# Sample projections by column groups, key/value weights in 16 KB runs, and buffer records split by later writes in an encoder step on eight cores

## The chip, the cores and the metric

The kernel runs on the 8 cores of one Trainium2 chip, in two dies of four. Each core works on its own data: no core waits for another. The metric is the device time of the slowest core, in microseconds (us). The shortened names in the profile are PE for TensorE (matmuls), PEld for its weight loads, DVE for VectorE, ACT for ScalarE, POOL for GpSimd and SP for SyncE.

## The reference

One step of an encoder layer is computed for two groups that share all weights: 4 prompt streams of 4096 frames, and 16 running streams of 16 frames each (the "sample" group, with pooling and convolution states and a cached memory). Cut to what matters here:

```python
def cross_attn(xn, mem_k, mem_v, w_q, w_co):
    q = jnp.einsum('btd,dhe->bthe', xn, w_q)
    s = jnp.einsum('bthe,bmhe->bhtm', q, mem_k).astype(jnp.float32) * (XHEAD_DIM ** -0.5)
    p = jax.nn.softmax(s, axis=-1).astype(mem_v.dtype)
    o = jnp.einsum('bhtm,bmhe->bthe', p, mem_v)
    return jnp.einsum('bthe,hed->btd', o, w_co)

def encoder_layer(x, ...):
    # 1: pooling and short gated convolution
    proj = rmsnorm(x, g_mix_pre) @ w_in                  # 1024 -> 2048
    ...
    x = x + rmsnorm(merged @ w_out, g_mix_post)
    # 2: cross-attention into 256 memory tokens, 4 heads of 256
    x = x + rmsnorm(cross_attn(rmsnorm(x, g_x_pre), mem_k, mem_v, w_q, w_co), g_x_post)
    # 3: squared-ReLU MLP, 1024 -> 4096 -> 1024
    hid = jnp.square(jax.nn.relu(rmsnorm(x, g_ff_pre) @ w_up))
    x = x + rmsnorm(hid @ w_down, g_ff_post)
# prompt group: mem_k = rmsnorm(mem) @ w_k and mem_v = rmsnorm(mem) @ w_v are computed and returned
```

Each core takes half a prompt stream (2048 frames) and two of the sample streams (32 rows).

## The kernel before, in words

**Tiling.** The 2048 prompt rows of a core are 4 tiles of 512 (`NT`, `TN`). Activations are held transposed in `xT` (feature chunks of 128 on the partitions), so a projection of 128 output features is 8 matmuls of a 128x128 weight block against 512 moving columns. The 32 sample rows ride along in the same way, transposed in `xTe`.

**Stages.** First comes the mixer for the four tiles, with the key/value projections of the memory (`kv_block(0..3)`, two halves of w_k, then two of w_v) put between the pooling groups of tile 2. Then w_q and the keys are folded into `Am` (`fold_a`) and the values and w_co into `Bm` (`fold_b`), and attention runs over the tiles in the order 2, 3, 0, 1. In the second of its four rounds `smp_q` and `smp_attn` do the sample rows. Last comes the MLP over tiles 0 to 3: 32 up chunks (`up_chunk`, 8 matmuls each, then ReLU on ACT and the square on DVE), then the down projection (`out_tile`, 32 chunks deep).

**Sample rows.** `smp_q` makes the queries as 8 output blocks of 128 features, each of 8 matmuls with a 128x128 block of w_q as weights and 32 moving columns. `up_smp(k, ps)` does the same for the four 128-feature chunks of w_up piece k, called after the four prompt chunks of piece k of tile 0, for all 8 pieces. The down projection and the two other output projections of the sample rows (`out_smp`) work the other way round: the 32 sample columns are the weights, 256 columns of the weight matrix move, and four such matmuls go to four groups of 32 array columns (PSUM partitions 0-31, 32-63, ...). Results there lie with 32 rows on 4 groups of partitions.

**Weights on the way.** w_up comes in 8 pieces of 1 MB (as bf16) into three slots `up0..2`. Piece k+3 goes into the slot of piece k and is issued once all its readers are done (`load_up`). The first four pieces of w_down are loaded before the MLP. The last four, `wdn4..7`, lie where attention had its buffers and are issued when piece 7 of w_up has landed (`load_down(4, 8, op)`). For tile 0 `out_tile` is called with `late`: it does the first half of the depth for two row blocks before it touches the second half. All these loads convert float32 to bf16 and are issued by POOL, in order. w_k and w_v come in two halves each into `wkv0` and `wkv1`, in runs of 512 floats (2 KB); the w_v halves are issued when the w_k half in the same buffer has been used.

**Order.** The engines' programs are written out by a planner. `Prog.add` records each operation with its reads and writes. `Tracker` holds a record for each write (its rectangle, its writer and those who read it since), and from overlaps the operation gets its dependences. A record is dropped when one later write covers it whole. `Prog.schedule` then lists the operations in order of time: on each engine, of those ready by its own cost figures, the one that comes first in the program. Its figure for DMAs is 280 GB/s for runs of 2 KB and 345 GB/s for runs of 16 KB (bytes of the float32 source), plus 2.6 us, and where several queues are active they share in proportion to their run length (2 KB counts 0.5, SP's 4 KB counts 1, 16 KB counts 4). The engines then run these lists in order, waiting only on semaphores.

**Lines.** Matmuls are recorded at L670, transposes at L675, ACT operations at L699, copies at L733 (ACT), L735 (DVE) and L737 (POOL), DVE operations at L706, L715, L720 and L725, and all DMAs at L744.

Of the kernel before, what the change touches and what calls it, by code (L numbers as in the profile page):

```python
# [7 lines left out]
F32 = mybir.dt.float32  # L8
BF16 = mybir.dt.bfloat16
F32R = mybir.dt.float32r  # L10
AF = mybir.ActivationFunctionType
ALU = mybir.AluOpType
# [3 lines left out]
D = 1024  # L16
# [6 lines left out]
NS = 32  # L23
# [172 lines left out]
class Prog:  # L196
# [9 lines left out]
    def add(self, opts, reads=(), writes=(), nbytes=0, lead=0, after=None, desc=4096):  # L206

        op = Op()
        op.idx = len(self.ops)
        op.opts = opts  # L210
        op.is_dma = nbytes > 0
        op.bytes = nbytes
        op.desc = desc
        op.deps = {} if after is None else {after: "raw"}
        op.prio = op.idx - lead
        op.ps_new = []
        op.ps_acc = set()
        op.eng = None
        self.ops.append(op)
        multi = len(opts) > 1  # L220
        eng = None if (op.is_dma or multi) else opts[0][0]

        def dep(p, kind):
            if p is not None and p is not op and op.deps.get(p) != "raw":
                op.deps[p] = kind
        for ap in list(reads) + list(writes):
            if isinstance(ap, PV):
                op.ps_acc.add(ap.ps)
                if ap.ps.id not in self.ps_seen:
                    self.ps_seen.add(ap.ps.id)  # L230
                    op.ps_new.append(ap.ps)
        for ap in reads:
            sp, rects = rects_of(ap)
            for r in rects:
                for rec in list(self.tr.find(sp, r)):
                    dep(rec.writer, "raw")
                    if sp[0] == "P":
                        for rd, k in rec.readers.items():
                            if k != eng or eng is None:
                                dep(rd, "war")  # L240
                    rec.readers[op] = eng
        for ap in writes:
            sp, rects = rects_of(ap)
            for r in rects:
                for rec in list(self.tr.find(sp, r)):
                    dep(rec.writer, "war")
                    for rd in rec.readers:
                        dep(rd, "war")
                    q = rec.rect
                    if r[0] <= q[0] and r[1] >= q[1] and r[2] <= q[2] and r[3] >= q[3]:  # L250
                        rec.dead = True
                self.tr.put(sp, r, op)
        return op

# [280 lines left out]
def build_program():  # L535
# [4 lines left out]
    def din(name, shape):  # L540
        return nc.dram_tensor(name, list(shape), F32, kind="ExternalInput")
# [10 lines left out]
    gd = {n: din(n, [1, D]) for n in gnames}  # L552
    win_d = din("w_in", [7, 128, 4096])
    wout_d = din("w_out", [128, 8192]); wco_d = din("w_co", [128, 8192])
    wk_d = din("w_k", [16, 128, 512]); wv_d = din("w_v", [16, 128, 512])
    wq_d = din("w_q", [16, 128, 512]); wqT_d = din("w_qT", [16, 128, 512])
    wup_d = din("w_up", [8, 128, 4096]); wdn_d = din("w_down", [8, 128, 4096])
    wpool_d = din("w_pool", [128, 512])
# [39 lines left out]
    rts = fix("rts", 16 * NS, BF16)  # L598
# [41 lines left out]
    wkv = [at("wkv%d" % i, W0 + i * 8192, 4096, BF16) for i in range(2)]  # L640
# [5 lines left out]
    wq = at("wq", A0 + 82 * K, 8 * D, BF16)  # L646
# [21 lines left out]
    def mm(out, lhsT, rhs, start, stop, share=1):  # L668
        n = ncols(rhs) / share
        P.add([("pe", lambda e, L: e.matmul(L(out), lhsT=lhsT, rhs=rhs, start=start, stop=stop,  # L670
                                            skip_group_check=True), max(0.03, n * 0.000421 + 0.001))],
              reads=[lhsT, rhs], writes=[out])

    def tr(out, in_, idn):
        P.add([("pe", lambda e, L: e.transpose(out=L(out), in_=in_, identity=idn),  # L675
                0.065 if in_.dtype == BF16 else 0.25)], reads=[in_, idn], writes=[out])
# [7 lines left out]
    def act(out, in_, func, scale=1.0, bias=None, accum=None, lead=0):  # L684
        rdl = [in_]
        wr = [out]
        kw = {}
        if bias is not None:
            kw["bias"] = bias
            rdl.append(bias)  # L690
        if not isinstance(scale, float):
            rdl.append(scale)
        if accum is not None:
            kw["accum_out"] = accum
            wr.append(accum)
        n = ncols(in_)

        def f(e, L):
            return e.activation(out=L(out), in_=L(in_), func=func, scale=scale, **kw)  # L699
        P.add([("act", f, c_act(n) + (0.19 if accum is not None else 0.0) + (0.06 if bias is not None else 0.0))], reads=rdl, writes=wr, lead=lead)  # L700

    def tt(out, in0, in1, op, eng="dve", per=1.0):
        n = ncols(out)
        opts = []
        if "dve" in eng:
            opts.append(("dve", lambda e, L: e.tensor_tensor(out=L(out), in0=L(in0), in1=L(in1), op=op), c_dve(n, per)))  # L706
        if "pool" in eng:
            opts.append(("pool", lambda e, L: e.tensor_tensor(out=L(out), in0=L(in0), in1=L(in1), op=op),  # L708
                         0.18 + n * 0.00168))
        P.add(opts, reads=[in0, in1], writes=[out])  # L710
# [18 lines left out]
    def copy(out, in_, eng="dve", per=1.0, after=None):  # L729
        n = ncols(out)  # L730
        opts = []
        if "act" in eng:
            opts.append(("act", lambda e, L: e.activation(out=L(out), in_=L(in_), func=AF.Copy, scale=1.0), c_act(n)))  # L733
        if "dve" in eng:
            opts.append(("dve", lambda e, L: e.tensor_copy(out=L(out), in_=L(in_)), c_dve(n, per)))  # L735
        if "pool" in eng:
            opts.append(("pool", lambda e, L: e.tensor_copy(out=L(out), in_=L(in_)), 0.18 + n * 0.002))  # L737
        return P.add(opts, reads=[in_], writes=[out], after=after)
# [10 lines left out]
    def load(out, in_, nbytes, q="sp", lead=LEAD, rd=False, after=None, desc=4096):  # L749
        return dma(q, out, in_, nbytes, rd=rd, lead=lead, after=after, desc=desc)  # L750

    def wload(dst, src, b0, b1, after=None):
        return load(dst.rearrange("p (b c) -> p b c", c=512), src[b0:b1].rearrange("b p c -> p b c"),
                    (b1 - b0) * 262144, q="pool", after=after, desc=2048)

    def r3(ap, n):
        return ap.rearrange("p (c t) -> p c t", c=n)
# [438 lines left out]


    def kv_loads(k, after=None):
        wload(wkv[k % 2][:, :], wk_d if k < 2 else wv_d, 8 * (k % 2), 8 * (k % 2) + 8, after)

    def kv_mem():
        for i in range(2):
# [55 lines left out]
    def attn_head(t, hh):  # L1258
# [16 lines left out]
            tt(p2, p2, r.unsqueeze(1).to_broadcast([128, 2, TN]), ALU.mult)  # L1275
        return finish

    def smp_loads():
        wload(kTs[:, :], ckT, 0, 8)
        wload(vSs[:, :], cv, 0, 8)  # L1280

    def smp_q():
        ps = PS(1)
        for j in range(8):
            for kc in range(8):
                mm(ps.v(0, 128, j * NS, (j + 1) * NS), wqk(j, kc), xTek(0, NS)(kc), kc == 0, kc == 7)
        copy(qTs[:, :], ps.v(0, 128, 0, 8 * NS), eng="act dve")

    def smp_attn():

# [31 lines left out]
    up_slot = {}  # L1322
# [14 lines left out]
        act(r, ps.v(0, 128, 0, TN), AF.Relu)  # L1337
        tt(hid(c), r, r, ALU.mult, per=0.5)

    def up_smp(k, ps):  # L1340
        s = up_slot[(0, k)]
        for jj in range(4):
            c = k * 4 + jj
            cl = c % 16
            for kc in range(8):
                mm(ps.v(0, 128, cl * NS, (cl + 1) * NS), s[:, jj * 1024 + kc * 128: jj * 1024 + (kc + 1) * 128],
                   xTek(0, NS)(kc), kc == 0, kc == 7)
        if k % 4 == 3:
            act(rts[:, :], ps.v(0, 128, 0, 512), AF.Relu)
            tt(hids[:, (k // 4) * 512:(k // 4 + 1) * 512], rts[:, :], rts[:, :], ALU.mult, per=0.5)  # L1350

    wd = lambda kc, h: dparts[kc // 4][:, (kc % 4) * D + h * 512: (kc % 4) * D + (h + 1) * 512]

# [123 lines left out]
            load_down(0, 4, xl[3])  # L1477
    load_gp("g_ff_post")
    load_gps(2)
    ups = None  # L1480
    for t in range(NT):
        for k in range(8):
            for jj in range(4):
                up_chunk(t, k * 4 + jj)
            if t == 0:
                if k % 4 == 0:
                    ups = PS(1)
                up_smp(k, ups)
            n = k + 3
            if n < 8:  # L1490
                op = load_up(t, n)
                if t == 0 and n == 7:
                    load_down(4, 8, op)
            elif t + 1 < NT:
                load_up(t + 1, n - 8)
        if t + 1 < NT:
            pre_tile(t + 1, 2, xT[(t + 1) % 2])
        out_tile(t, hid, 32, wd, gslot["g_ff_post"], yp, late=t == 0)
        if t == 0:
            out_smp(lambda kc: hids[:, kc * NS:(kc + 1) * NS], 32, wd)  # L1500
            dma("sp", ysm[:, :], Xs[:, :], NS * 4096, wr=False)
        if t + 2 < NT:
            load_tile(t + 2, x2)
# [117 lines left out]
```

How the kernel before makes its waits and increments, by code:

```python
        def run(e, eng):  # L474
            seen = {}
            ends = sorted(dma_last.items(), key=lambda kv: kv[1].end)
            for n, op in enumerate(seqs[e]):
                if e == "sp" and n == len(seqs[e]) - 1:
                    for k, last in ends:
                        if last.end < op.start - SETTLED and seen.get(k, 0) < last.semval:
                            eng.wait_ge(dsem[k], last.semval)
                            seen[k] = last.semval
                waits = {}
                for p in plan[op]:
                    k, v = (p.sem, p.semval) if p.is_dma else (p.eng, p.sigval)
                    if seen.get(k, 0) >= v:
                        continue
                    if waits.get(k, 0) < v:
                        waits[k] = v
                for k, v in waits.items():
                    eng.wait_ge(dsem[k] if isinstance(k, tuple) else esem[k], v)
                    seen[k] = v
                ins = op.fn(eng, lambda x: x.resolve(psum) if isinstance(x, PV) else x)
                if op.is_dma:
                    ins.then_inc(dsem[op.sem], 16)
                elif op.needs_signal:
                    ins.then_inc(esem[e], 1)
            if e == "sp":
                for k, last in ends:
                    if seen.get(k, 0) < last.semval:
                        eng.wait_ge(dsem[k], last.semval)
```

## Time and profile before

| | |
|---|---|
| device time, median of 3 runs | 848.71 us (848.17 to 849.42) |
| profiled execution, device time | 848.66 us |
| its span (slowest core, core 6) | 847.1 us |
| spans of the eight cores | 841.2 to 847.1 us |
| PE busy | 813.7 us (96%) |
| DVE, ACT, POOL busy | 391.1, 390.8, 102.2 us |
| HBM read, written by the core | 144.38 MB, 18.07 MB |

The profiled execution lies 0.05 us under the median of the runs, so its rows can be set against it directly. Its device time is 1.5 us more than its span. A busy figure for PE is the union of matmuls in flight; a single matmul of 512 columns is shown as 379 ns long, while one starts every 0.216 us.

### The profile page before, as it was taken

Reading aid. Unit: us, or ns where it says so; the run is one execution under the profiler, and the core shown is the slowest. Engines: PE = TensorE matmul, PEld = TensorE weight load, DVE = VectorE, ACT = ScalarE, POOL = GpSimd, SP = SyncE. Lnnn points to the kernel's source line nnn. Section 1 sums busy time; section 2 is a strip of 40 time slices with the busy share of each in tenths; the row PEclk is TensorE's granted clock in tenths of the full one; section 3 lists DMA queues with packets and bytes.
Section 4 is the critical chain, followed back from the end, with each engine's and each line's share of the span. In section 5 each row is a group of like instructions: output and inputs, shape, how many; then the busy total and the mean of one; then the engine's idle time right before and its main releaser. Section 6 shows DMA issues by size and latency. Waiting matters only on the chain.

```text
span 847.1 us, 13900 instructions; the slowest of 8 cores (841.2 to 847.1 us)
## 1 busy us (share of the span) xinstructions
PE 813.7 (96%) x4708; PEld 391.2 (46%) x4708; DVE 391.1 (46%) x540; ACT 390.8 (46%) x806; POOL 102.2 (12%) x179
## 2 busy tenths in 40 slices
PE   3889999899999999999999999999999999999997
PEld 1444454444644454455454454444444444444443
DVE  4886885568966666765222222241222321222112
ACT  3586786758867556675332233332233411233101
POOL 7612103002111113110010000000000000000000
PEclk9999999999999999999999999999999999999999
DMA  9999439550396606993889716881248820185011
GB/s 196 199 229 202 129 117 208 111 81 1 65 149 113 199 26 187 161 174 84 149 144 165 186 72 132 154 147 53 99 96 156 156 68 26 50 150 100 1 50 50
DMA packets 29793, 102.39 MB, mean 121 GB/s; under 512 B 2386, under 2 KB 13266, under 8 KB 24348
## 3 DMA queue, kind: packets, MB, share of 16 engines
q0 software_dynamic: 19408, 67.32, 46.4%
q1 hardware_dynamic: 9740, 32.75, 11.5%
q10 hardware_dynamic: 576, 1.44, 0.5%
q8 instruction: 39, 0.64, 0.3%
q14 instruction: 30, 0.25, 0.1%
HBM read 144.38 MB, written 18.07 MB: 192 GB/s over the span
## 4 chain that ended last, share of the span: by engine, by line
PE 83%; DMA 11%; DVE 2%; issue 2%; POOL 1%; ACT 1%; another core or an unknown queue 0%; DVEq 0%; ACTq 0%; POOLq 0%
PE ps L670 80%; DMA X<-xp 4%; DMA wdn<-w_down 4%; PE ps L675 2%; DMA wkv<-w_v 2%; DMA up<-w_up 1%; POOL win L744 0%; DVE X L725 0%; ACT junk L699 0%; POOL wdn L744 0%; DVE O L706 0%; DVE z L725 0%; DVE z L706 0%; DVE V L706 0%
## 5 line engine op out<-in xcount | busy, mean ns | idle before, releaser
L670 PE MATMUL ps<-wdn,hid 128*128 128x512 bf16 x1024 | 222.3, 379 | 0.7 <-DMA wdn<-w_down 0.7
L670 PE MATMUL ps<-xT,up 128*128 128x512 bf16 x1024 | 222.6, 379 | 0.0
L670 PEld LDWEIGHTS ps<-wdn,hid 128*128 128x128 bf16 x1024 | 99.9, 98 | 120.4 <-issue 1.2
L670 PEld LDWEIGHTS ps<-xT,up 128*128 128x128 bf16 x1024 | 99.7, 98 | 119.1 <-issue 0.2
L706 DVE TENSOR_TENSOR O<-ps,gp 128x1024 f32<-128x1024 f32 (+1 forms) x49 | 58.3, 1200 | 191.0 <-PE ps L670 122.0
L699 ACT ACTIVATE rt<-ps 128x512 bf16<-128x512 f32 x128 | 76.4, 597 | 142.2 <-PE ps L670 138.3
L670 PE MATMUL ps<-xT,win 128*128 128x512 bf16 x512 | 122.1, 384 | 13.5 <-DMA win<-w_in 12.6
L706 DVE TENSOR_TENSOR hid<-rt 128x512 bf16<-128x512 bf16 x128 | 54.4, 425 | 157.8 <-ACT rt L699 156.0
L699 ACT ACTIVATE sqj<-ps 128x1024 bf16<-128x1024 f32 (+1 forms) x33 | 32.8, 994 | 173.2 <-PE ps L670 171.0
L670 PEld LDWEIGHTS ps<-xT,win 128*128 128x128 bf16 x512 | 49.4, 98 | 71.6 <-issue 17.7
L725 DVE SCALAR_TENSOR_TENSOR X<-O,st,X 128x1024 f32<-128x1024 f32 (+1 forms) x49 | 62.8, 1294 | 4.6 <-DVE O L706 3.8
L744 POOL DMA_DIRECT2D up<-w_up x32 | 17.2, 539 | 378.5 <-PE ps L670 364.9
L706 DVE TENSOR_TENSOR xT<-ps,cst 128x1024 bf16<-128x1024 bf16 x44 | 53.1, 1219 | 20.4 <-PE ps L675 20.2
L670 PE MATMUL ps<-wout,mg 128*128 128x512 bf16 x256 | 58.1, 379 | 3.3 <-DMA wout<-w_out 2.6
L699 ACT ACTIVATE xs<-X 128x1024 bf16<-128x1024 f32 x40 | 41.9, 1050 | 35.4 <-DMA X<-x 31.7
L670 PE MATMUL ps<-xT,Am 128*128 128x512 bf16 x256 | 58.3, 379 | 0.0
L670 PE MATMUL ps<-Bm,mg 128*128 128x512 bf16 x256 | 58.2, 379 | 0.0
L670 PEld LDWEIGHTS ps<-wout,mg 128*128 128x128 bf16 x256 | 24.6, 98 | 31.7 <-issue 3.9
L670 PEld LDWEIGHTS ps<-xT,Am 128*128 128x128 bf16 x256 | 24.2, 98 | 28.5 <-issue 1.7
L670 PEld LDWEIGHTS ps<-Bm,mg 128*128 128x128 bf16 x256 | 24.1, 98 | 27.2 <-issue 0.8
L708 POOL TENSOR_TENSOR psm<-mg 128x512 fp32r<-128x512 bf16 x16 | 19.3, 1208 | 108.8 <-ACT st L699 69.5
L675 PEld LDWEIGHTS ps<-idb,xs 128*128 128x128 bf16 (+1 forms) x412 | 26.2, 98 | 10.2 <-issue 2.0
(184 smaller groups left out, 687.1 us busy)
## 6 DMA issues: line engine op xcount, KB each, us to landing
up<-w_up POOLq DMA_DIRECT2D x32, 1024.0 KB, 9.9
x<-X SPq DMA_DIRECT2D x16, 512.0 KB, 4.2
X<-x SPq DMA_DIRECT2D x16, 512.0 KB, 4.5
wdn<-w_down POOLq DMA_DIRECT2D x8, 1024.0 KB, 30.0
yp<-X SPq DMA_DIRECT2D x15, 512.0 KB, 2.7
X<-xp POOLq DMA_DIRECT2D x8, 512.0 KB, 44.5
X<-xp SPq DMA_DIRECT2D x8, 512.0 KB, 4.4
win<-w_in POOLq DMA_DIRECT2D x4, 768.0 KB, 26.9
```

Of the source, the lines that this page charges most:

```text
L670: P.add([("pe", lambda e, L: e.matmul(L(out), lhsT=lhsT, rhs=rhs, start=start, stop=stop, skip_group_check=True), max(0.03, n * 0.000421 + ...
L675: P.add([("pe", lambda e, L: e.transpose(out=L(out), in_=in_, identity=idn), 0.065 if in_.dtype == BF16 else 0.25)], reads=[in_, idn], wri ...
L699: return e.activation(out=L(out), in_=L(in_), func=func, scale=scale, **kw)
L706: opts.append(("dve", lambda e, L: e.tensor_tensor(out=L(out), in0=L(in0), in1=L(in1), op=op), c_dve(n, per)))
L708: opts.append(("pool", lambda e, L: e.tensor_tensor(out=L(out), in0=L(in0), in1=L(in1), op=op), 0.18 + n * 0.00168))
L725: return P.add([("dve", lambda e, L: e.scalar_tensor_tensor(out=L(out), in0=L(in0), scalar=scalar, in1=L(in1), op0=op0, op1=op1), c_dve(nc ...
L744: return P.add([(q, lambda e, L: e.dma_start(out=out, in_=in_), 0.5 + nbytes / desc * 0.0005 if q == "pool" else 0.43)], reads=[in_] if rd ...
```

## The change

Four edits:

1. `smp_q` takes the queries in column groups: 8 depth steps of 4 matmuls (32 sample columns as weights, 256 moving columns of w_q, one group of 32 array columns for each head). The 128x256 result is copied to `rts[:, 0:256]`, turned by two 128x128 transposes (new function `turn_blocks`) and copied to `qTs`.
2. `up_smp(k)` does the same for pieces k and k+1 of w_up together, and is called after the prompt chunks of piece k for even k. So it reads slot k+1 as well, before the prompt chunks of piece k+1. ReLU and square are done on the 128x256 result, two transposes and a copy put it into `hids`.
3. w_k and w_v are stored as [2, 128, 4096], and each half is loaded in runs of 16 KB (4096 floats a partition) by `load` instead of `wload`.
4. In `Prog.add`, a write in SBUF that covers all rows of a record and some of its columns drops the record, and puts records for the columns left of it and right of it, with the old writer and the old readers.

```diff
-                    if r[0] <= q[0] and r[1] >= q[1] and r[2] <= q[2] and r[3] >= q[3]:
+                    if r[0] <= q[0] and r[1] >= q[1] and (sp[0] == "S" or r[2] <= q[2] and r[3] >= q[3]):
                         rec.dead = True
+                        for lo, hi in ((q[2], r[2]), (r[3], q[3])):
+                            if lo < hi:
+                                self.tr.put(sp, (q[0], q[1], lo, hi), rec.writer).readers.update(rec.readers)
...
-    wk_d = din("w_k", [16, 128, 512]); wv_d = din("w_v", [16, 128, 512])
+    wk_d = din("w_k", [2, 128, 4096]); wv_d = din("w_v", [2, 128, 4096])
...
     def kv_loads(k, after=None):
-        wload(wkv[k % 2][:, :], wk_d if k < 2 else wv_d, 8 * (k % 2), 8 * (k % 2) + 8, after)
+        load(wkv[k % 2][:, :], (wk_d if k < 2 else wv_d)[k % 2], 2097152, q="pool", after=after, desc=16384)
...
+    def turn_blocks(rows, dst):
+        ps = PS(1)
+        for q in range(2):
+            tr(ps.v(0, 128, q * 128, (q + 1) * 128, BF16), rows[:, q * 128:(q + 1) * 128], idb[:, :])
+        copy(dst.rearrange("p (g q t) -> p g q t", g=4, q=2),
+             ps.v(0, 128, 0, 256, BF16, lambda a: a.rearrange("p (q g t) -> p g q t", q=2, g=4)), eng="act dve")
...
     def smp_q():
         ps = PS(1)
-        for j in range(8):
-            for kc in range(8):
-                mm(ps.v(0, 128, j * NS, (j + 1) * NS), wqk(j, kc), xTek(0, NS)(kc), kc == 0, kc == 7)
-        copy(qTs[:, :], ps.v(0, 128, 0, 8 * NS), eng="act dve")
+        for kc in range(8):
+            for hh in range(4):
+                w = r3(wq[:, :], 8)[:, 2 * hh:2 * hh + 2, kc * 128:(kc + 1) * 128]
+                mm(ps.v(32 * hh, 32 * hh + 32, 0, 256, F32, lambda a: r3(a, 2)), xTek(0, NS)(kc), w, kc == 0, kc == 7, share=3)
+        q = rts[:, 0:256]
+        copy(q, ps.v(0, 128, 0, 256), eng="act dve")
+        turn_blocks(q, qTs[:, :])
...
-    def up_smp(k, ps):
-        s = up_slot[(0, k)]
-        for jj in range(4):
-            ...
+    def up_smp(k):
+        ps = PS(1)
+        for kc in range(8):
+            for g in range(4):
+                w = r3(up_slot[(0, k + g // 2)][:, :], 4)[:, 2 * (g % 2):2 * (g % 2) + 2, kc * 128:(kc + 1) * 128]
+                mm(ps.v(32 * g, 32 * g + 32, 0, 256, F32, lambda a: r3(a, 2)), xTek(0, NS)(kc), w, kc == 0, kc == 7, share=3)
+        r, h = rts[:, 0:256], rts[:, 256:512]
+        act(r, ps.v(0, 128, 0, 256), AF.Relu)
+        tt(h, r, r, ALU.mult, per=0.5)
+        turn_blocks(h, hids[:, k * 128:(k + 2) * 128])
...
-            if t == 0:
-                if k % 4 == 0:
-                    ups = PS(1)
-                up_smp(k, ups)
+            if t == 0 and k % 2 == 0:
+                up_smp(k)
```

## Rows read from the trace of the kernel before

**Rows 1.** The page: busy time, and PE's granted clock in 40 slices.
```profile
PE 813.7 (96%) x4708; PEld 391.2 (46%) x4708; DVE 391.1 (46%) x540; ACT 390.8 (46%) x806; POOL 102.2 (12%) x179
...
PEclk9999999999999999999999999999999999999999
```
**Rows 2.** Span and mean granted clock of the cores: two of the eight.
```profile
core 3: 845.2 us, clock 0.997
...
core 6: 847.1 us, clock 1.000
```
**Rows 3.** Who PE waited for, core 6: total us, times, longest us.
```profile
PE ps L670 <- DMA win<-w_in: 12.9, 2, 12.6
PE ps L670 <- DMA wout<-w_out: 2.6, 1, 2.6
PE ps L670 <- DMA wkv<-w_v: 2.2, 2, 2.0
...
PE ps L670 <- DMA wdn<-w_down: 0.7, 1, 0.7
```
**Rows 4.** Groups of instructions by form: busy us, mean ns | idle before.
```profile
L670 PE MATMUL ps<-xTe,up 128*128 128x32 bf16 x256 | 7.7, 176 | 0.0
```
**Rows 5.** Timeline of PE: start us, us until the last end, count; sample products.
```profile
412.65 0.96 PE L670 MATMUL ps<-xTe,up 128*128 128x32 bf16 x32
413.46 7.07 PE L670 MATMUL ps<-xT,up 128*128 128x512 bf16 x32
...
312.71 5.77 PE L670 MATMUL ps<-Bm,mg 128*128 128x512 bf16 x26
318.41 1.06 PE L670 MATMUL ps<-wco,mgs 128*32 128x256 bf16 x32
319.40 0.82 PE L670 MATMUL ps<-xT,Am 128*128 128x512 bf16 x3
...
502.35 3.68 PE L670 MATMUL ps<-wdn,hids 128*32 128x256 bf16 x128
505.96 1.68 PE L670 MATMUL ps<-xT,up 128*128 128x512 bf16 x7
```
**Rows 6.** Timeline of all engines at the start of the MLP.
```profile
382.98 1.97 PE L670 MATMUL ps<-xTe,up 128*128 128x32 bf16 x72
383.04 1.21 DVE L706 TENSOR_TENSOR xT<-ps,cst 128x1024 bf16<-128x1024 bf16 x1
...
384.80 0.38 PE L670 MATMUL ps<-xT,up 128*128 128x512 bf16 x1
```
**Rows 7.** The chain that ended last: the two DMAs in tile 0's MLP.
```profile
422.29 9.16 DMA up<-w_up
...
434.14 31.72 DMA wdn<-w_down
```
**Rows 8.** Timeline of PE around these two DMAs.
```profile
421.18 7.07 PE L670 MATMUL ps<-xT,up 128*128 128x512 bf16 x32
...
450.64 14.62 PE L670 MATMUL ps<-wdn,hid 128*128 128x512 bf16 x67
466.00 19.37 PE L670 MATMUL ps<-wdn,hid 128*128 128x512 bf16 x89 [0.73 <-DMA wdn<-w_down]
```
**Rows 9.** Timeline of POOL: issues of w_up pieces 3 and 4.
```profile
394.01 0.58 POOL L744 DMA_DIRECT2D up<-w_up  x1 [25.04 <-PE ps L670]
399.44 0.53 POOL L744 DMA_DIRECT2D up<-w_up  x1 [4.86 <-PE ps L670]
```
**Rows 10.** Timeline of POOL and PE: the w_v loads and their first readers.
```profile
129.25 0.95 POOL L744 DMA_DIRECT2D wkv<-w_v  x1 [22.91 <-PE ps L670]
...
137.76 0.91 POOL L744 DMA_DIRECT2D wkv<-w_v  x1 [0.55 <-PE ps L675]
...
148.56 3.61 PE L670 MATMUL ps<-wkv,mT 128*128 128x512 bf16 x16 [0.18 <-DMA wkv<-w_v]
...
158.50 3.61 PE L670 MATMUL ps<-wkv,mT 128*128 128x512 bf16 x16 [2.00 <-DMA wkv<-w_v]
```

More of the change, by code:

```diff
@@ L1338, in up_chunk @@
         tt(hid(c), r, r, ALU.mult, per=0.5)
-    def up_smp(k, ps):
-        s = up_slot[(0, k)]
-        for jj in range(4):
[L1343 to L1350, printed above, removed]
+    def up_smp(k):
[8 more added lines that the diff above has]
+        turn_blocks(h, hids[:, k * 128:(k + 2) * 128])
     wd = lambda kc, h: dparts[kc // 4][:, (kc % 4) * D + h * 512: (kc % 4) * D + (h + 1) * 512]
@@ L1479, in build_program @@
     load_gps(2)
-    ups = None
     for t in range(NT):
@@ L1548, in oct, with sides @@
         return f(a.reshape(128, 8, 4096).transpose(1, 0, 2))
+    def sides(w):
+        return f(chunks(f(w).reshape(D, D), 512).reshape(128, 2, 4096).transpose(1, 0, 2))
     def blk(a):
@@ L1558 @@
         "w_out": f(rows(w_out[0])).reshape(128, -1),
-        "w_k": blk(chunks(f(w_k[0]).reshape(D, D), 512)), "w_v": blk(chunks(f(w_v[0]).reshape(D, D), 512)),
+        "w_k": sides(w_k[0]), "w_v": sides(w_v[0]),
         "w_q": blk(chunks(f(w_q[0]).reshape(D, D), 128)),
```

## The prediction

> **What bounds the kernel now.** I read the page first: PE is busy for 813.7 of 847.1 us and at full clock (2.4 GHz) in every slice, while ACT and DVE are under half [rows 1]. So PE's list is the spine, and the question for each edit is whether PE's next wait moves with it. Then the cores: the slowest is core 6, 1.9 us behind core 3 [rows 2]. Then who PE waited for on core 6 [rows 3]: 12.9 us for the first w_in pieces, which no edit touches, 2.6 us for w_out, 2.2 us for w_v and 0.7 us for w_down. These last three, 5.5 us together, are what sets core 6 behind the best cores. Last the chain of waits, which shows that within the MLP of tile 0 two DMAs and not PE carry the time: w_up piece 7 for 9.16 us and then the last four w_down pieces until 465.9 us [rows 7]. After that PE runs without a wait to the end.
>
> The sums below are made against the profiled execution: device time 848.66, of which 847.1 is core 6's span and 1.5 lies around it. The runs' median is 848.71, so nothing is converted.
>
> **Edit 1, the sample queries.** The old form: 32 matmuls of 32 columns take from 412.65 to 413.46, 0.81 us or 25.3 ns each [rows 5]. `smp_q` has 64: 1.62 us. The new form stands in the trace as the w_co product of the sample rows, 32 matmuls of 256 columns in four column groups: from 318.41 to 319.40. A full matmul of 512 columns starts every 0.2158 us ((14.62 - 0.379)/66 of the 67 in rows 8; one is shown 0.379 us long). The 26 ahead of the group start at 312.71 and are through at 318.32, so the group costs 1.08 us [rows 5]. I add two transposes of 128 columns, a quarter of a full matmul each (54 ns), 0.11 us. New 1.19 us, saved 0.43 us. The copy, the second copy and the wait between them lie on ACT and DVE; the attention products behind them have 28 and more ready matmuls of the prompt in front of them. If that cover were gone it would cost about 1.5 us once. Attention is PE-bound here, so I count 0.43 us in full.
>
> The longer group of the same form, 128 matmuls, takes 3.61 us [rows 5]. Two equations (0.99 = 32x + c, 3.61 = 128x + c) give x = 27.3 ns and c = 0.12 us, and 0.09 us are lost on entering. So a group pays some 0.2 us for going in and out. The Trainium skill (TensorEngine Tiling, "Key Properties") says that changing the tiling mode drains TensorE; the trace agrees, with these 0.2 us. Without the drain five new groups would be 1.0 us cheaper; I use the row, which contains it.
>
> **Edit 2, the sample up products.** 256 matmuls [rows 4] at 25.3 ns are 6.5 us. The new form is four groups at 1.19 us, 4.8 us. PE has 1.7 us less to do. Whether that is time depends on where.
>
> (a) Ahead of the MLP. 72 of the small matmuls stand between 382.98 and 384.80 while `xT` for tile 0 is being finished: DVE's last piece ends at 383.04 + 1.21 = 384.25 and the first prompt chunk starts at 384.80 [rows 6]. With one group of at most 1.08 us for pieces 0 and 1 PE is done by about 384.1 and then waits for `xT`, until about 384.38. The MLP starts 0.42 us earlier, and the rest of what is saved there is idle time.
>
> (b) From there to the release of the slot of piece 4, which lets w_up piece 7 be issued. Before: 384.80 to 421.18, 36.4 us [rows 6, 8]: 160 prompt matmuls (34.5 us) and the 73 small ones of pieces 2 to 4 (1.85). After: 34.5 us, the groups for pieces 2 and 3 and for 4 and 5 (2.16) and four transposes (0.22), 36.9 us. That is 0.5 us more, since pieces 0 to 2 were done ahead of the MLP before and piece 5 is now done ahead of the release. So the release moves by +0.5 - 0.42 = +0.1 us.
>
> (c) From the release PE's need and the DMA run a race. DMA: piece 7 lands at 431.45, the four w_down pieces are issued then, and the last has landed at 465.9, 44.8 us after the release, during which the loads are back to back (31.7 us for four, some 8 us each) [rows 7]. PE: 44.1 us, from 421.18 until it stands at 465.27 with 88 down matmuls done and waits 0.73 us [rows 8]. In the new kernel three sets of small ones go (3 x 0.81 = 2.43), one group and four transposes come (1.08 + 0.22): 43.0 us, 1.1 us less. The DMA part is the same. So the wait for w_down grows from 0.7 to about 1.9 us, and everything saved behind the release is lost to it. Behind 466 the work is the same as before.
>
> So edit 2 gives -0.1 us net (a loss of 0.1 on its own, bounds -0.5 to +1.7 saved, the latter if the DMAs shrink with PE). The new reads of slot k+1 cost nothing by the rows: piece 5's slot is free at about 384.4 + 20.7 + 1.1 = 406.2, the load is issued 0.8 us later and lands 9.2 us after that (as piece 7 did [rows 7]), at 416.2; its first reader, the group behind piece 4, starts at about 420.1. Cover gone, it would cost the difference.
>
> **Edit 3, key/value weights.** POOL's issue of such a load is 0.95 us in runs of 2 KB and 0.53 to 0.58 in runs of 16 KB [rows 9, 10]; POOL is 12% busy, so that is nothing. The w_k halves are last in POOL's queue at 20 us and first used at 124: nothing. The w_v halves are issued at 129.25 and 137.76 and land just before 148.56 and 158.50, 19.3 and 20.7 us later, beside stores and loads of X on SP's queue [rows 10]. A lone 16 KB load of this size takes 9.16 us [rows 7]. If only the landing moved, 2.2 us of waits would go. But PE's list moves too. PE came to the two blocks 19.1 and 18.7 us after the issues (148.38 and 156.50, taking off the waits), which is where the planner, with its 280 GB/s and a share of a third against SP, expected them. With 345 GB/s and a share of four fifths it expects them about 10.5 us after the issue, so it puts the blocks at about 139.8 and 148. The first load lands between 9.2 us (alone) and 19.3 us (as now) after its issue; by the nearest row, the 9.16 us one, stretched by X's traffic, I take 11 us, 140.3. The second cannot start until the first is through: about 8 us later plus some of X's traffic, 148 to 152, I take 149.8. PE then waits some 2 us in all (bounds 0 and 10), against 2.2 us now: 0.2 us gained. Cores without such a wait before (core 3 is one) get about 1 us of it, and stay under core 6.
>
> **Edit 4, the tracking.** It removes dependences only. An example: an old record of the first stage reaches from `rt0` into the slot `up0`, so loads into `up0` also wait for the readers of `rt`. Piece 3 is issued at 394.01, 2.3 us after its chunk's matmuls ended (384.80 + 32 x 0.2157 = 391.7), piece 4, in `up1`, only 0.8 us after its own (398.6) [rows 9]. The load comes up to 1.5 us earlier, but PE waits for no w_up piece [rows 3], and piece 7 lies in `up1`. The same in attention and between the two `rt` buffers: ACT and DVE have slack. I take 0, with 1 us to either side, because the planner's lists are made anew and small shifts follow.
>
> **Sum.** -0.43 (edit 1) + 0.1 (edit 2) - 0.2 (edit 3) + 0 = -0.55 us: **848.1 us**. What a measurement of this kernel can tell from no change is 0.2%, 1.7 us, so this is "within".
>
> **Rivals.** (A) *Everything saved counts.* The DMA chain of the MLP gives way with PE, and w_v is in time: -0.43 - 1.7 - 2.2 = -4.3 us on core 6. Core 3 has no w_v wait and saves only 2.1, and becomes the slowest at 843.1 + 1.5: 844.6 us. For it: core 6 is slowest by DMA waits alone [rows 2, 3]. Against it: between 434 and 466 the DMAs run back to back [rows 7], and PE's list follows the planner.
> (B) *The w_v blocks are put too early, the slower side.* Place: kv_block(2) and (3). X's stores and loads on SP take as much of the DMAs as now, and w_v lands at about 144 and 153 while PE comes at 139.8 and 148: 5 us of waits for 2.2 now, on every core. 848.1 + 3.0 = 851.1 us. It decides from 4.5 us of waits in all, where the time leaves 0.2%. For it: the planner's figure for 16 KB loads is short, 6.1 us of transfer where the w_down pieces took about 8 [rows 7]; for 2 KB loads the sharing made up for it. The Trainium skill (DMA: Bandwidth & Descriptors, "Queues, rings and completion order") says that each DMA engine takes its queues in turn by packets. By that rule SP would not be pushed back to a fifth, and this rival would gain; no row here shows the turns.
> (C) *The change does not do what it says for PE*: a group of four column tiles, with moving operands in two pieces of 128 columns, runs at half the pace of the rows, 60 ns a matmul. Then each group costs 0.9 us more; of the five those of the queries, of the first pieces (0.6 of it) and the two in (b) count, 3.3 us: 851.4 us. Against it: the rows for both out-products, which differ only in having one piece.
> (D) *The new lists* happen to shift POOL's psum additions or the w_down issues by one or two us, to either side: 846 or 850 us.
>
> **Numbers.** Forecast 0.47. A (all or most of it) 0.25, B 0.16, C 0.02, D 0.10, of which 0.05 on the fast side, 0.04 on the slow side and 0.01 inside the 0.2%. Faster is 0.25 + 0.05 = 0.30, slower 0.16 + 0.02 + 0.04 = 0.22, within 0.48. The range reaches into A and B: 844.7 to 851.0. The forecast's own is 846.8 to 849.6.
>
> **What would show it.** Sample groups of 32 matmuls in about 1.0 to 1.1 us with four of them in the MLP and one in attention. PE's first prompt chunk of the MLP right after DVE's last `xT` piece. PE's wait for w_down at about 1.9 us on core 6, and present on cores that had none or little. PE reaching the w_v blocks about 10 us after the issues, and waits for them on most cores. The forecast is wrong if w_down's wait does not grow, if the w_v waits are gone or above 4 us, or if PE shows a wait of over 1 us in a place not named here.

## The result, and the profile after

The changed kernel takes 854.13 us (median of 7 runs; 852.13 and up) where the kernel before takes 848.60 (7 runs, 848.17 to 849.45): the ratio is 1.0057 [1.0046, 1.0068], 4.8 us slower. One run of the seven (879.67 us) had one die at a lower clock from end to end and is left out of the ratio, and on the first two chips of the experiments below one die was like that in every run, so that their table compares die 0 as well, over the runs in which that die is undisturbed, and e5 to e8 have no ratio. The forecast was 848.1 with a range up to 851.0. It was wrong, on the slow side.

The profiled run took 854.79 us. Its page (busy time and instructions; share of the chain of waits), against [rows 1]:

```profile
PE 811.1 (95%) x4472; PEld 389.2 (46%) x4558; DVE 393.7 (46%) x544; ACT 391.2 (46%) x811; POOL 99.4 (12%) x179
...
PE 85%; DMA 9%; DVE 2%; issue 2%; ACT 1%; POOL 1%; another core or an unknown queue 0%; ACTq 0%; DVEq 0%; POOLq 0%
```

PE has 2.6 us less to do and the kernel takes about 5 us more, so the loss is idle time or clock. The cores, as in [rows 2]:

```profile
core 3: 852.8 us, clock 0.993
core 4: 853.2 us, clock 0.990
...
core 7: 846.7 us, clock 0.994
```

Six of the eight cores (spans from 846.0 to 853.2) are later than the 847.1 of the slowest before. The mean granted clock is 0.990 to 0.998, where it was 0.996 to 1.000. Who PE waited for on core 4, as in [rows 3]:

```profile
PE ps L673 <- DMA win<-w_in: 15.5, 2, 14.8
PE ps L673 <- DMA wkv<-w_v: 3.4, 1, 3.4
PE ps L673 <- ACT st L702: 2.1, 1, 2.1
PE ps L673 <- DMA wdn<-w_down: 1.6, 1, 1.6
```

Two rows are the news. The wait for w_v was on three cores before (2.0, 2.2 and 1.0 us) and is on all eight now (5.2, 3.4, 5.4, 3.4, 3.4, 5.2, 2.1, 2.0). And `ACT st` was no row of before at all; it is on six cores now, with 1.0 to 2.1 us.

**Where it arises.** I took four points on every core, and the means over the cores: the first matmul of the `wkv` blocks is 1.5 us later than before, the first `Am` product (about 245 us before) 5.8 us later, the first prompt chunk of the MLP 5.4, the end 5.9. So nearly all is lost ahead of 251 us, and most of it in the stage with the key and value blocks. The w_v loads and their first reader there, POOL and then PE of core 4 (compare [rows 10]):

```profile
133.59 0.60 POOL L747 DMA_DIRECT2D wkv<-w_v  x1 [24.47 <-PE ps L673]
...
142.31 0.57 POOL L747 DMA_DIRECT2D wkv<-w_v  x1
```
```profile
143.94 0.38 PE L673 MATMUL ps<-pld,wpool 128*128 128x512 bf16 x1
147.71 4.66 PE L673 MATMUL ps<-wkv,mT 128*128 128x512 bf16 x14 [3.40 <-DMA wkv<-w_v]
```

Taking off the wait, PE came at 144.3, 10.7 us after the issue. The chain has the load itself:

```profile
133.59 13.98 DMA wkv<-w_v
```

And the 14 matmuls behind the wait take until 152.21, 4.5 us where 3.0 is their pace at full clock. The busy time of the engines in steps of 2 us shows why; the column after POOL is the granted clock (PE, PEld, DVE, ACT, POOL busy, clock, DMA share, GB/s):

```profile
144.00:146.00 2.00, 0.31 (x2) 0.00 (x0) 0.58 (x1) 2.00 (x4) 0.00 (x0) 1.00 0.95 207
146.00:148.00 2.00, 0.29 (x1) 0.14 (x2) 1.90 (x3) 0.37 (x1) 0.50 (x1) 0.83 1.08 291
148.00:150.00 2.00, 2.00 (x6) 0.73 (x5) 0.16 (x1) 0.00 (x0) 0.21 (x1) 0.50 0.97 166
150.00:152.00 2.00, 2.00 (x10) 0.78 (x8) 0.00 (x0) 0.68 (x2) 0.00 (x0) 0.82 1.14 174
152.00:154.00 2.00, 2.00 (x12) 0.94 (x11) 0.76 (x2) 1.74 (x3) 0.00 (x0) 1.00 0.97 209
```

The clock goes to 0.50 (1.2 GHz) as PE comes out of the wait and is back at 1.00 (2.4 GHz) by 152: six matmuls in two microseconds, where the last row has twelve. The Trainium skill (TensorE: Matmul & The Clock Gate, "Part 1") describes a clock gate with just these two levels, which goes to the lower one when PE has stood idle; the trace agrees, since the steps at 0.83 and 0.82 are the ones in which it switched.

The wait of 2.1 us for `ACT st` stands earlier. ACT and PE of core 4:

```profile
88.11 1.06 ACT L702 ACTIVATE xs<-O 128x1024 bf16<-128x1024 f32 x1 [2.98 <-DMA O<-mem]
```
```profile
91.40 0.38 PE L673 MATMUL ps<-sq,ones 128*128 128x512 bf16 x1 [2.15 <-ACT st L702]
```

ACT's list now has the square of the memory rows ahead of their landing. ACT stands 2.98 us, the work of the gates is queued behind it, and PE waits for that. The experiments with the planner's new figure (e1, e5, e7, e9, e10, below) have this wait on some of their cores too; the kernel before and the experiments with the old figure have it on none.

**The account, means over the cores.** Between 120 and 170 us PE is idle 3.85 us where it was 0.86: +3.0. The clock of that stretch was 1.00 on every core and is 0.97 on six cores and 0.93 on two; of 50 us that is 1.7 and 3.4, mean 2.1, a little of which lies inside the waits. Ahead of it +1.5. Between 170 and 240 the idle time falls from 1.9 to 0.35: −1.5. And the new list has six matmuls of 512 columns more (`ps<-wco,vT`) and ten transposes fewer between the first `wkv` matmul and the first `Am` product: +0.75, a shift and not a loss. Together +5.9 for the 5.8 found.

### The profile page after: what moved, and what is told of

It is laid out like the page before. It is cut to its first block, busy times and chain, and to the rows that moved or that the text cites. A ratio compares the mean times of both kernels' runs of the same rounds, so it can differ in the third digit from the quotient of the medians.

```text
span 853.2 us, 13491 instructions; the slowest of 8 cores (846.0 to 853.2 us)
## 1 busy us (share of the span) xinstructions
PE 811.1 (95%) x4472; PEld 389.2 (46%) x4558; DVE 393.7 (46%) x544; ACT 391.2 (46%) x811; POOL 99.4 (12%) x179
## 4 chain that ended last, share of the span: by engine, by line
PE 85%; DMA 9%; DVE 2%; issue 2%; ACT 1%; POOL 1%; another core or an unknown queue 0%; ACTq 0%; DVEq 0%; POOLq 0%
PE ps L673 82%; DMA wdn<-w_down 4%; DMA win<-w_in 3%; PE ps L678 2%; DMA wkv<-w_v 2%; DMA up<-w_up 1%; DVE mg L709 0%; DVE sAB L1048 0%; DVE O L709 0%; DVE X L728 0%; DVE pld L728 0%; ACT sq L702 0%; POOL win L747 0%; ACT rf L702 0%
## 5 line engine op out<-in xcount | busy, mean ns | idle before, releaser
L673 PEld LDWEIGHTS ps<-wdn,hid 128*128 128x128 bf16 x1024 | 99.9, 98 | 121.2 <-issue 2.1
L673 PE MATMUL ps<-xT,win 128*128 128x512 bf16 x498 | 122.6, 390 | 16.3 <-DMA win<-w_in 14.8
L678 PEld LDWEIGHTS ps<-idb,xs 128*128 128x128 bf16 (+1 forms) x412 | 26.3, 98 | 10.5 <-issue 1.6
L678 PE MATMUL ps<-idb,xs 128*128 128x128 bf16 (+1 forms) x412 | 30.6, 218 | 0.0
```

## The experiments

Twelve runs, in three sets of four on one chip each (e1 to e4, e5 to e8, e9 to e12), beside the kernel before. The last column compares the slowest core of die 0: the difference of the means to the kernel before beside it, with its 95% interval.

| | what | device us, before beside it | ratio | die 0, slowest core, us |
|---|---|---|---|---|
| e1 | edit 3 alone | 856.39, 855.06 | 1.0017 [0.9999, 1.0036] | +3.83 [3.08, 4.72] |
| e2 | edit 4 alone | 854.33, 855.06 | 0.9994 [0.9978, 1.0009] | −0.32 [−1.11, 0.47] |
| e3 | edits 1 and 2 | 855.58, 855.06 | 1.0005 [0.9988, 1.0022] | −1.57 [−2.04, −1.04] |
| e4 | edit 3, old figure to the planner | 854.93, 855.06 | 1.0008 [0.9994, 1.0022] | −1.22 [−1.72, −0.70] |
| e5 | old loads, new figure | 872.93, 866.31 | | +10.40 [9.27, 11.53] |
| e6 | all but edit 3 | 863.24, 866.31 | | −0.35 [−1.55, 0.72] |
| e7 | all but edit 4 | 866.93, 866.31 | | +2.48 [1.55, 3.44] |
| e8 | all, old figure | 861.41, 866.31 | | −1.61 [−2.49, −0.77] |
| e9 | all, again | 852.15, 848.52 | 1.0044 [1.0032, 1.0056] | +3.96 [3.08, 4.91] |
| e10 | all, PE kept busy in the wait | 852.39, 848.52 | 1.0044 [1.0028, 1.0059] | +4.01 [2.8, 5.1] |
| e11 | edits 1 to 3, old figure | 845.97, 848.52 | 0.9969 [0.9956, 0.9981] | −2.37 [−2.89, −1.85] |
| e12 | edit 1 alone | 848.92, 848.52 | 1.0004 [0.9992, 1.0016] | +0.61 [−0.41, 1.72] |

**Which edit.** e1 takes from the change the two `w_k`/`w_v` declarations, `sides` and the one line of `kv_loads`; e2 the tracker alone; e3 `smp_q`, `up_smp` and `turn_blocks` alone.

> The kernel before with edit 3 alone (key/value weights in 16 KB runs, loaded by load, planned with 345 GB/s and share 4). Theory P (place): PE's list puts the two w_v blocks some 8 us sooner, the loads come only 1 to 4 us sooner; waits for w_v of 2 to 5 us on every core, a clock fall to half speed behind them that costs 1.5 us or more; 851.5 to 853 us. Theory L (the 16 KB loads themselves disturb the rest, on SP's queue above all): the same time here, so this run does not part P from L. Theory T (the loss is edit 4's): 847 to 849 us, no wait above those of before.

> The kernel before with edit 4 alone (records split by later writes). Theory P: the w_v blocks stay where they were, so no w_v wait above 2.2 us; new lists shift small waits in 80 to 120 us and 330 to 380 us, 848.5 to 850.5 us. Theory T: edit 4 carries most of the loss, 852 us or more.

> The kernel before with edits 1 and 2 alone (column groups for the sample queries and up products). By the terms of the prediction: -0.4 us for the queries, +0.1 for the MLP, the wait for w_down grown by about 1.1 us: 848.2 us. Rival C (a group in column tiles at half the pace): 851 us or more.

Edit 3 alone makes the loss. On each core of e1 PE waits for w_v, from 2.0 to 4.4 us. The clock has little part in it here: in the profiled execution it fell on core 0 alone, and the fall that was expected on every core did not come. Core 4, the first w_v block and the steps of 2 us behind the wait:

```profile
144.55 2.53 PE L670 MATMUL ps<-wkv,mT 128*128 128x512 bf16 x11 [3.31 <-DMA wkv<-w_v]
```
```profile
144.00:146.00 2.00, 1.45 (x7) 0.71 (x8) 0.43 (x2) 0.00 (x0) 0.33 (x1) 1.00 1.05 193
146.00:148.00 2.00, 2.00 (x12) 0.88 (x9) 0.00 (x0) 1.32 (x3) 0.00 (x0) 1.00 0.94 201
```

Edit 4 alone is nothing that can be measured, and edits 1 and 2 gain 1.6 us.

**The loads, or the list?** Edit 3 does two things: it changes the runs in memory, and it tells the planner 16,384 bytes a descriptor, from which the planner works out when a load is through and where the readers stand in the lists. e4 has the new runs and the old number:

```diff
-        load(..., 2097152, q="pool", after=after, desc=16384)
+        load(..., 2097152, q="pool", after=after, desc=2048)
```

Its PE, DVE, ACT and SP have the instructions of the kernel before in the same order. e5 is the other half: weights as before, the same 2 KB runs, in one load with the new number.

```diff
-        wload(wkv[k % 2][:, :], wk_d if k < 2 else wv_d, 8 * (k % 2), 8 * (k % 2) + 8, after)
+        load(wkv[k % 2][:, :].rearrange("p (b c) -> p b c", c=512),
+             (wk_d if k < 2 else wv_d)[8 * (k % 2):8 * (k % 2) + 8].rearrange("b p c -> p b c"),
+             2097152, q="pool", after=after, desc=16384)
```

> The kernel before with the 16 KB runs of edit 3, but the planner is given the old figure (2 KB) for these four loads, so that the lists of all engines stay those of before, line by line. Theory P: loads that come sooner under an unchanged list can only take waits away; the w_v waits of up to 2.2 us go, 846.5 to 848.6 us. Theory L: 850 us or more with an unchanged list.

> The kernel before, its w_k and w_v loads in 2 KB runs as they were, but the planner told 16 KB (345 GB/s, share 4) for them: only the lists change, to those of edit 3 alone. Theory P (place): PE comes to the w_v blocks as early as with edit 3 and the loads come later still; +5 to +9 us against before on the undisturbed die, w_v waits of 6 to 10 us. Theory L (16 KB loads): no loss, within 1 us of before.

First PE's first w_v block and the time of the loads on core 3 of e4, then on core 3 of e1 the waits and the time of the loads:

```profile
147.30 3.62 PE L670 MATMUL ps<-wkv,mT 128*128 128x512 bf16 x16
...
DMA to landing us min/median/max: 12.3/12.8/13.4
```
```profile
PE ps L670 <- DMA wkv<-w_v: 4.1, 2, 2.9
...
DMA to landing us min/median/max: 13.4/13.8/14.2
```

The same loads take nearly the same time (12.3 to 14.8 us on the cores of e4, 12.3 to 14.5 in e1; 17.0 to 20.5 with 2 KB runs before). In e4 PE comes 18.9 us after the issue (128.4 on this core) and waits on no core; in e1 it comes early and waits. With the old loads at the early places, core 3 of e5:

```profile
151.97 4.34 PE L670 MATMUL ps<-wkv,mT 128*128 128x512 bf16 x11 [9.32 <-DMA wkv<-w_v]
...
DMA to landing us min/median/max: 17.0/18.4/19.7
```

Here the wait is 9.3 us and the slowest core of die 0 is 10.4 us later; a part of that is clock, which is 0.90 to 0.93 between 120 and 170 us on the cores of die 0. So the number in the planner's hand does the harm, 5 us of it between e4 and e1, and the shorter landing mends a part of it: 10.4 (e5) to 3.8 us (e1), measured on two chips.

**All together, without one.** e6 leaves out edit 3, e7 edit 4, and e8 keeps all four with the old number.

> The changed kernel without edit 3 (column groups and new tracking, key/value loads as before). Theory P: the loss goes with edit 3; on the undisturbed die -1.5 us against before (edits 1 and 2 alone measured that) with up to 1 us to either side for edit 4's lists. Rival I (edit 4 costs 2 to 3 us once the column groups are in, whatever the loads do): +1 us or more.

> The changed kernel without edit 4 (column groups and 16 KB key/value loads, old tracking). If the edits add up: +3.6 - 1.5 = +2.1 us on the undisturbed die. If edit 4 is what makes the whole worse than that sum (the whole stands at some +4.5), this one lies 2 us under the whole.

> The changed kernel with one number undone: the planner is told 2 KB runs for the key/value loads (280 GB/s, share 0.5), the loads stay in 16 KB runs. Theory P: PE comes to the w_v blocks late enough again, no w_v wait above 1 us and no clock fall behind it; -1.5 to -2.5 us against before on the undisturbed die. Rival I (edit 4's lists cost by themselves): above before.

Without edit 3 (e6), or with it and the old number (e8), the loss is gone; without edit 4 it stays (e7). The sizes do not quite add up. The single edits give +3.8 − 1.6 − 0.3 = +1.9, e7 agrees with that (+2.5), but the whole in e9 has +4.0, the case that its expectation took for a sign that edit 4 and the early blocks harm each other. That is not settled: e7 and e9 ran on different chips and their intervals overlap.

**The clock.** e10 puts 14 matmuls, whose result the block then overwrites, ahead of the first w_v block, so that PE works through most of the wait:

```diff
+    def busy(e, L):
+        for _ in range(14):
+            i = e.matmul(L(out), lhsT=mT[:, 0:128], rhs=mT[:, 0:512], start=True, stop=True, ...)
+    P.seqs["pe"].insert(P.seqs["pe"].index(first), d)
```

> The changed kernel as it is, on the chip of the three runs beside it. Sum of the single edits on the undisturbed die: +3.8 (edit 3) -1.6 (edits 1 and 2) -0.3 (edit 4) = +2.0 us. If they add up: +2 us. If edit 4's lists and the early w_v blocks harm each other: +4 us or more, as the first comparison of the whole (5.5 us on the slowest core) suggests.

> The changed kernel with 14 matmuls of 512 columns more on PE, right ahead of the first w_v block, on operands that are there (their result is written over): 3.0 us of work in place of the 2 to 5 us of waiting there. Everything else stays line by line. Theory G (the wait is paid twice, since PE's granted clock halves behind it): the clock stays at 1.0 in 140 to 160 us and the time falls by 1 to 2 us against the changed kernel. Rival (only the wait itself counts): the same time, or up to 1 us slower on cores that wait less than 3 us.

PE's timeline and the steps of 2 us in e10, core 5:

```profile
142.01 3.19 PE L1530 MATMUL ps<-mT 128*128 128x512 bf16 x14
145.35 3.18 PE L673 MATMUL ps<-wkv,mT 128*128 128x512 bf16 x14 [0.16 <-DMA wkv<-w_v]
```
```profile
146.00:148.00 2.00, 2.00 (x11) 0.93 (x10) 0.02 (x1) 0.60 (x1) 0.07 (x1) 1.00 1.12 180
148.00:150.00 2.00, 2.00 (x12) 0.94 (x11) 0.71 (x2) 1.66 (x3) 0.00 (x0) 1.00 1.04 197
```

The clock stays at 1.00 and the 14 matmuls take 3.0 us again; on none of the eight cores does the clock of 120 to 170 us fall, where in e9 it is 0.97 on five. But the time is the same, as the rival in the expectation had it, and the 1 to 2 us of theory G did not come. The sum is nearly even: 14 matmuls of 0.215 us are 3.0 us and 1.1 us of waits for w_v remain, 4.1; in e9 there are 3.3 us of waits and, five cores of eight at 0.97 over 50 us, 1.1 us of clock, 4.4. From the first `wkv` matmul to the first `Am` product a core takes 123.6 us in the mean in e10 and 123.9 in e9, as this sum would have it, but the time of whole runs does not resolve it.

The cores of e9 do show what a fall costs. Cores 0 and 7 run the same list and wait 2.66 us each:

```profile
143.89 4.80 PE L673 MATMUL ps<-wkv,mT 128*128 128x512 bf16 x14 [2.47 <-DMA wkv<-w_v]
```
```profile
140.27 3.18 PE L673 MATMUL ps<-wkv,mT 128*128 128x512 bf16 x14 [1.38 <-DMA wkv<-w_v]
...
149.92 0.59 PE L673 MATMUL ps<-wkv,mT 128*128 128x512 bf16 x2 [1.28 <-DMA wkv<-w_v]
```

On core 0 the clock of 120 to 170 us is 0.97, on core 7 it is 1.00, and the stretch to the first `Am` product takes 123.8 and 122.2 us. Core 1, with 2.8 us of waits and the clock at 1.00, takes 122.4. So one fall costs about 1.5 us.

**A version that beats both, and edit 1 by itself.** e11 is edits 1, 2 and 3 with `desc=2048` and the old tracking. e12 is edit 1 alone.

> The kernel before with edits 1, 2 and 3, but the planner told 2 KB for the key/value loads, and the old tracking: the lists are those of edits 1 and 2 alone. If gains add: -1.6 and -1.2, so -2 to -2.8 us against before on the undisturbed die, the best version so far. If the 16 KB loads only remove waits that the slowest core had: -1.6 us.

> The kernel before with edit 1 alone (sample queries in column groups). By the prediction's term -0.4 us; then the MLP part has given 1.0 of the 1.4 to 1.6 us that edits 1 and 2 measured together, where the prediction had +0.1. Rival: the queries give 1 us or more, as the prediction's wait for w_down eats the MLP's part.

e11's slowest core, and PE's sample group and resumption after w_down on core 6 of it:

```profile
core 6: 844.8 us, clock 0.998
```
```profile
382.65 7.07 PE L670 MATMUL ps<-xT,up 128*128 128x512 bf16 x32 [0.33 <-DVE xT L706]
...
418.58 1.06 PE L670 MATMUL ps<-up,xTe 128*32 128x256 bf16 x32
419.57 1.90 PE L670 MATMUL ps<-xT,up 128*128 128x512 bf16 x8
...
463.78 16.56 PE L670 MATMUL ps<-wdn,hid 128*128 128x512 bf16 x76 [1.22 <-DMA wdn<-w_down]
```

e11 is 2.6 us faster than the kernel before and 6.2 faster than the changed one. No core of it waits for w_v: from the first `wkv` matmul to the first `Am` product all eight take 120.1 to 120.2 us. Before, that stretch took 120.2 to 120.4 on the five cores without a wait and 121.4 to 122.7 on the three with one, and in e9 it takes 122.2 to 125.7.

## Why the prediction was wrong

**Edit 3 is the step that failed**, in three places. The arrival of PE was right: "about 10.5 us after the issue", measured 10.7. The landing was mis-sized: I took 11 us "by the nearest row, the 9.16 us one", and it took 14.0 on core 4 and 11.7 to 15.5 over all. The nearest row was that of a load without X's traffic beside it; the rows of the same place, 19 to 21 us with 2 KB runs [rows 10], were the better anchor, and the middle of the two would have been 14 to 15. The wait of "some 2 us in all" became 2.0 to 5.4 on each core, inside the stated bounds of 0 and 10, which the sum did not use; the cores without a wait before were to get about 1 us and stay under core 6. Second, the clock: a wait was counted at its own length, but the matmuls behind it ran at half pace for a while on all eight cores, at about 1.5 us a fall. Third, "PE's list moves too" was applied to the blocks and not to ACT's share in `kv_mem`, which moved ahead of its own load and cost PE 1.0 to 2.1 us at 90 us on six cores.

**Rival B was what happened**, by place and mechanism: the blocks too early, on every core, with the planner's figure for 16 KB runs as the cause. It named 5 us of waits and "decides from 4.5"; measured mean 3.8 of w_v waits, so by its price alone the time would have stayed within 0.2%. The fallen clock and ACT's wait, which it did not have, go with the rest, up to 854 for its 851.1. It had a chance of 0.16. What spoke for it, a planner that expects 6.1 us where loads of this size took 8 [rows 7], was a row about this kernel. What spoke for my 11 us was an assumption on X's traffic. X's traffic did give way, but less than the planner's four fifths ask: on cores 0, 4 and 6 the last X load beside the first w_v load took 20.1 to 21.0 us, where it took 12.5 to 14.7, and w_v still took 12.3 to 14.0. No run shows the turns of the queues themselves.

**Edit 1** is 0.43 in the text. e12 gives +0.61 [−0.41, 1.72], which neither shows nor excludes it; attention from its first to its last `Am` product went from 118.04 to 117.80 in the mean. A group of 32 takes 0.99 us from start to start in e11, and its two transposes 0.11, both as taken. Rival C is out: its groups would be 0.9 longer.

**Edit 2.** (a) was right: in e11 PE waits 0.33 us for DVE's last piece of `xT` (text 0.28), and the MLP starts 18.3 to 18.6 us after the last `Am` product of attention, for 18.7 to 19.0 (−0.4; text 0.42). (b) was right: from there to the release 36.9 us in e11 (382.65 to 419.57), the text's number. In the changed kernel it is 37.7, since its new lists put 19 of the first 32 behind the first chunk, and the MLP starts 17.1 us after the last `Am` product. (c) was half right. The changed kernel, core 4, PE and then the chain (compare [rows 7, 8]):

```profile
426.62 1.06 PE L673 MATMUL ps<-up,xTe 128*32 128x256 bf16 x32
...
455.97 14.62 PE L673 MATMUL ps<-wdn,hid 128*128 128x512 bf16 x66
472.24 7.93 PE L673 MATMUL ps<-wdn,hid 128*128 128x512 bf16 x35 [1.64 <-DMA wdn<-w_down]
```
```profile
428.49 8.12 DMA up<-w_up
438.83 33.28 DMA wdn<-w_down
```

From the release at 427.6 PE needs until 470.6, 43.0 us, exactly as worked out, and the wait of 1.6 is near the 1.9. What failed is "the DMA part is the same". Before and in e12 the cores that wait have their last w_down piece 44.8 to 45.8 us after the release (one core of e12 44.1); with edit 2 it is 43.9 to 44.8 in e11 and 43.3 to 44.6 in the changed kernel, about 1 us less, the way that the bound "if the DMAs shrink with PE" allowed. Why the four loads go faster stays open. And half the cores never wait for w_down: in e11 their MLP of tile 0 takes 119.7 us for 120.3, and that of the four that wait 121.2 in the mean for 121.6. With the start, edit 2 gives −0.7 to −1.0 where the sum had +0.1, and e3's −1.57 stands against the −0.33 of edits 1 and 2.

**Edit 4** was right at 0: e2 gives −0.32 [−1.11, 0.47].

**The signs named in advance** worked in part: "a wait of over 1 us in a place not named" came in with ACT's, and w_v waits "above 4 us" on three cores of eight (5.2 to 5.4), though not on the slowest, core 4, with 3.4.

## What to carry to other kernels

Where an order is fixed ahead of time from a cost model, a faster transfer is two changes, the bytes and the planner's number for them, and they can be measured apart by giving the one without the other; here the transfer gained 1.2 us and the number cost 5. The number should be the landing in the company that the load has in that place, not the one of the load alone. A new PE wait can cost more than its length, because the clock may fall behind it: a fall cost about 1.5 us here. It is a chance and not a rule, since it came on all cores of the changed kernel, on five of eight in e9 and on one of eight in e1, with waits of much the same size.

## What the runs showed of the hardware

A wait of 2.12 us can be enough for the clock to fall. Core 2 of e12, the matmuls behind the wait and the steps of 2 us around it:

```profile
151.81 2.49 PE L670 MATMUL ps<-wkv,mT 128*128 128x512 bf16 x6 [2.12 <-DMA wkv<-w_v]
154.52 2.59 PE L670 MATMUL ps<-wkv,mT 128*128 128x512 bf16 x9 [0.22 <-issue]
```
```profile
152.00:154.00 2.00, 2.00 (x6) 0.68 (x5) 0.00 (x0) 0.00 (x0) 0.00 (x0) 0.52 1.23 205
154.00:156.00 2.00, 1.78 (x6) 0.78 (x6) 0.69 (x1) 0.00 (x0) 0.00 (x0) 0.63 0.56 96
```

That core took 124.2 us for the stretch that takes 120.2 without a wait: 4.0 us for 2.1 us of waiting for w_v, 2.8 us of idle time in all. Core 6 of the kernel before waited 2.2 us in two waits, the longer 2.0, kept the clock at 1.00 and took 122.7: 2.5 us lost. A longer wait did not always bring the fall: cores 1 and 4 of e1 stood 3.0 and 3.3 us in one piece, and core 6 of e10 3.05, with the clock at 1.00 throughout. So the same wait is paid once or with about 1.5 us on top, by what the clock does.
